# One fused two-layer block on one core: gain rows and x loaded differently at the start, work moved across four chunk boundaries, output stored by chunks

## The chip, the cores and the metric

The kernel runs on one core of one Trainium2 chip. The metric is the device time of one execution in microseconds (us), the median of several runs. One launch computes the whole function.

## What is computed

Two blocks follow each other on a 256 x 2048 float32 activation. The first block has one wide input projection, two attention branches (MLA and differential), a gated merge, an output projection, and a PEER layer with 16384 experts. The second block has an even mixer (retention and a short convolution) and an odd mixer (windowed attention with sinks).

```python
h = rmsnorm(x, g_norm1[l]);  proj = h @ w_in[l]
y_a = mla_branch(proj, ...) @ w_o_mla[l]
y_b = diff_branch(proj, ...) @ w_o_diff[l]
merged = gates[..., :D_MODEL] * y_a + gates[..., D_MODEL:] * y_b
x = x + merged @ w_out[l]
x = x + peer_ffn(rmsnorm(x, g_norm2[l]), w_q_peer[l], sub_keys[l], expert_u[l], expert_v[l])
x = rmsnorm(x, g_final)
# second block
x = x + even_mixer(rms_norm(x, ev_norm_w[0]), ev_w_in[0], ev_conv_w[0], ev_w_out[0], pos)
x = x + odd_mixer(rms_norm(x, od_norm_w[0]), od_w_in[0], ..., od_w_out[0], pos)   # qk-norm, rope, gate = silu
```

## The kernel before

All weights are streamed once, as 1025 blocks of 128 x 1024 float32 (512 KB; the eight blocks of `w_narrow` are 128 x 640), in the order of the table `STREAM`: `w_narrow`, `w_att`, `w_gate`, `w_uq`, `w_ukv`, `w_ob`, `w_oa`, `w_out`, `w_qp`, `w_u`, `w_v`, `w_ein`, `w_eout`, `w_oin`, `w_oout`. SyncE's queue (SP) issues the loads into four `raw` slots. A slot is loaded again once VectorE has read it.

Every block goes through the same chain, which keeps float32 precision. ScalarE writes `hi` (the block rounded to fp32r, L1047), VectorE writes `lo` = raw - hi (L1464), each in two halves, and TensorE multiplies hi*hi, lo*hi and hi*lo (L589, L590, L591): 12 matmuls of 512 columns for a block. There are two `hi`/`lo` slots, so ScalarE can split block b+1 only when TensorE has left block b-1. The activations stand transposed in `xt`, also as hi and lo. They come from TensorE transposes of pairs of tiles (`turn_pair`, L559), and ScalarE and VectorE take them out of the bank (`plain_pair`, or `gain_pair` with the norm's gain, L1082 and L1524).

Each of the engines runs one list that is written out by hand. `gemm` walks over the chunks (512 output columns) and over the blocks of a chunk. VectorE's `take` moves a finished chunk out of its two banks, and adds 1 to `chunk_out`. All other work (norms, rope, softmax, gates) is placed by `beside...(slot)` between two splits; `slot` counts the blocks. `feed(q)` places the takes of transposed pairs, and `LATE` names the pairs that only exist once a chunk has been finished.

The places that the change touches are these. At the start TensorE waits for the identity matrix and all five rows of norm gains, which GpSimd's queue (POOL) loads, and transposes the gains (L703). Then pairs 0 to 2 of x are turned and the eight blocks of `w_narrow` follow; beside them ScalarE squares x for the norm (L1117), one token tile of 128 x 2048 at slot 2 and one at slot 4. In `w_oa`, VectorE's `take_a` runs four operations at each of four chunk ends (L1830, L1831). Between `w_ein` and `w_eout`, and between `w_oin` and `w_oout`, ScalarE applies Silu to the last chunk and VectorE multiplies it in (L1689) ahead of its next split. In `w_oin`, TensorE turns the keys (`turn_qk`, L980) after blocks 14 and 15, into one bank, and VectorE copies them out (`take_qk`, L2233) at its slots 16 and 17. VectorE's slot s stands behind its split of block s+1. At the end, the whole output (2 MB) is stored by one transfer from GpSimd's queue (L467).

```python
if slot in (14, 15):                 # TensorE, beside_oin
    if slot == 14:
        pe.wait_ge(tm_ready, ready.next())
    turn_qk(pairs("swa")[8 + slot - 14])
if slot in (16, 17):                 # VectorE, beside_oin
    take_qk(8 + slot - 16)
```

## Time and profile before

| | |
|---|---|
| median of 3 runs | 3107.28 us (3105.11 to 3108.09) |
| the profiled execution | 3105.93 us |
| its span in the trace | 3103.9 us |
| TensorE matmuls busy | 3052.5 us (98%) |
| VectorE, ScalarE, GpSimd busy | 2024.4 us (65%), 1501.4 us (48%), 567.7 us (18%) |
| mean DMA rate | 189 GB/s |

The profiled execution took 2.0 us more than its span, which the trace does not see. It lies 1.35 us below the median of the runs. Times below are counted from the span's start.

### The profile page before, as it was taken

The page shows a single profiled execution, that of the slowest core. Times are in us where ns is not written, and L with a number is a line of the kernel's source. Part 1 is how long each engine was busy: PE and PEld are TensorE (multiplying, and loading weights), DVE is VectorE, ACT ScalarE, POOL GpSimd, SP SyncE. Part 2 cuts the span into 40 slices and gives each one's busy share as a digit, 9 for nine tenths or more (in the row PEclk, how much of TensorE's full clock was granted, in tenths as well). Part 3 has the DMA queues.
Part 4 walks back from the last instruction along what each step waited for, and adds up shares of the span by engine and source line. Part 5 has one row for each costly group of instructions (what it writes and reads, how often), then busy time and mean ns, then how long its engine had stood idle before and what let it go on. Part 6 is the DMA issues. An engine that isn't in the chain of part 4 may idle for free.

```text
span 3103.9 us, 44769 instructions
## 1 busy us (share of the span) xinstructions
PE 3052.5 (98%) x14773; PEld 2493.2 (80%) x14773; DVE 2024.4 (65%) x3615; ACT 1501.4 (48%) x2443; POOL 567.7 (18%) x341
## 2 busy tenths in 40 slices
PE   7999999999999999999999999999999999999998
PEld 6888787788888888888877777777778888877787
DVE  4567677656877777655555555555576676568864
ACT  4445464455545454544444444444464445556553
POOL 1000000000088878887000000000000000000000
PEclk9999999999999999999999999999999999999999
DMA  6877554466577777776666666676666555653355
GB/s 227 251 258 241 166 163 142 159 187 206 170 183 180 182 183 183 182 185 189 222 224 210 209 206 213 209 231 202 187 191 192 176 170 177 198 167 122 110 157 167
DMA packets 197194, 587.97 MB, mean 189 GB/s; under 512 B 54608, under 2 KB 54736, under 8 KB 195776
## 3 DMA queue, kind: packets, MB, share of 16 engines
q1 hardware_dynamic: 148688, 537.99, 55.7%
q0 software_dynamic: 48368, 48.20, 7.5%
q8 instruction: 80, 1.31, 0.2%
q14 instruction: 58, 0.48, 0.0%
HBM read 565.00 MB, written 21.10 MB: 189 GB/s over the span
## 4 chain that ended last, share of the span: by engine, by line
PE 57%; DVE 1%; issue 0%; ACT 0%; POOL 0%; DVEq 0%; ACTq 0%
PE bank L884 8%; PE bank L589 8%; PE bank L886 8%; PE bank L885 8%; PE bank L591 8%; PE bank L590 8%; PE bank L814 6%; PE bank L815 3%; PE bank L654 1%; PE bank L559 1%; PE bank L666 0%; DVE lo L1464 0%; PE bank L676 0%; PE bank L677 0%; PE bank L675 0%
## 5 line engine op out<-in xcount | busy, mean ns | idle before, releaser
L1464 DVE TENSOR_TENSOR lo<-raw,hi 128x512 fp32r<-128x512 f32 (+2 forms) x1530 | 1313.6, 870 | 930.6 <-ACT hi L1047 920.1
L1047 ACT ACTIVATE hi<-raw 128x512 fp32r<-128x512 f32 (+2 forms) x1530 | 1181.7, 775 | 1482.4 <-PE bank L591 638.4
L814 PE MATMUL bank<-xt,hi 128*128 128x512 f32 x2304 | 818.8, 399 | 5.5 <-DVE lo L1464 4.8
L589 PE MATMUL bank<-hi,xt 128*128 128x512 f32 (+1 forms) x1924 | 768.2, 399 | 13.9 <-DVE lo L1464 13.6
L591 PE MATMUL bank<-hi,xt 128*128 128x512 f32 (+1 forms) x1924 | 751.4, 391 | 0.0
L590 PE MATMUL bank<-lo,xt 128*128 128x512 f32 (+1 forms) x1924 | 749.8, 390 | 0.0
L815 PE MATMUL bank<-xt,lo 128*128 128x256 f32 x2304 | 645.2, 280 | 0.0
L435 POOL DMA_INDIRECT gates_scratch<-picked,place x256 | 507.6, 1983 | 257.2 <-DVE picked L1961 148.9
L814 PEld LDWEIGHTS bank<-xt,hi 128*128 128x128 f32 x2304 | 432.2, 188 | 123.0 <-issue 18.8
L589 PEld LDWEIGHTS bank<-hi,xt 128*128 128x128 f32 x1924 | 363.7, 189 | 96.6 <-issue 21.8
L815 PEld LDWEIGHTS bank<-xt,lo 128*128 128x128 f32 x2304 | 434.9, 189 | 0.0
L591 PEld LDWEIGHTS bank<-hi,xt 128*128 128x128 f32 x1924 | 363.1, 189 | 76.9
L590 PEld LDWEIGHTS bank<-lo,xt 128*128 128x128 f32 x1924 | 364.0, 189 | 69.8
L884 PE MATMUL bank<-hi,w_hi 128*128 128x512 f32 x1024 | 406.7, 397 | 1.9 <-issue 1.8
L886 PE MATMUL bank<-hi,w_lo 128*128 128x512 f32 x1024 | 406.0, 397 | 0.0
L885 PE MATMUL bank<-lo,w_hi 128*128 128x512 f32 x1024 | 405.1, 396 | 0.0
L884 PEld LDWEIGHTS bank<-hi,w_hi 128*128 128x128 f32 x1024 | 192.2, 188 | 81.2 <-DVE lo L1464 42.1
L886 PEld LDWEIGHTS bank<-hi,w_lo 128*128 128x128 f32 x1024 | 192.7, 188 | 46.4
L885 PEld LDWEIGHTS bank<-lo,w_hi 128*128 128x128 f32 x1024 | 193.2, 189 | 35.5
L445 POOL DMA_DIRECT2D xt<-gates_scratch x31 | 23.2, 751 | 569.8 <-DVE hall L1660 506.3
L467 POOL DMA_DIRECT2D out<-hall x1 | 0.7, 717 | 456.4 <-DVEq L2337 456.4
L394 POOL DMA_DIRECT2D hall<-in_q_norm x1 | 0.5, 540 | 377.5 <-DVEq L2213 377.5
(215 smaller groups left out, 1657.8 us busy)
## 6 DMA issues: line engine op xcount, KB each, us to landing
raw<-in_w_u SPq DMA_DIRECT2D x256, 512.0 KB, 3.6
raw<-in_w_v SPq DMA_DIRECT2D x256, 512.0 KB, 3.6
raw<-in_w_ein SPq DMA_DIRECT2D x128, 512.0 KB, 4.0
raw<-in_w_oin SPq DMA_DIRECT2D x72, 512.0 KB, 3.6
raw<-in_w_att SPq DMA_DIRECT2D x64, 512.0 KB, 4.3
raw<-in_w_gate SPq DMA_DIRECT2D x64, 512.0 KB, 3.8
gates_scratch<-u_low POOLq DMA_DIRECT2D x16, 1024.0 KB, 7.6
raw<-in_w_out SPq DMA_DIRECT2D x32, 512.0 KB, 3.9
```

The costliest lines, as they stand in the source:

```text
L435: gp.indirect_dma_start(cells, bass.IndirectOffsetOnAxis(ap=place[:, c:c + 1], axis=0), picked[:, c:c + 1], None, compute_op=ALU.add).then ...
L559: mm = pe.transpose(dst[:, k * T + t * P:k * T + t * P + P], tile[t], ident[:, :])
L589: pe.matmul(acc, xh, h_[:, s], start=first, stop=False)
L590: pe.matmul(acc, xh, l_[:, s], start=False, stop=False)
L591: mm = pe.matmul(acc, xl, h_[:, s], start=False, stop=last)
L814: pe.matmul(acc[:, :], h_[:, s], xt[:, tile].rearrange("p w t -> p (w t)"), start=first, stop=False)
L815: return pe.matmul(acc[:, 0:T], l_[:, s], xt_hi[:, tile], start=False, stop=last)
L884: pe.matmul(acc, wh, h_[:, s], start=first, stop=False)
L885: pe.matmul(acc, wh, l_[:, s], start=False, stop=False)
L886: mm = pe.matmul(acc, wl, h_[:, s], start=False, stop=last)
L1047: act.activation(hi[d][:, c], raw[s][:, c], ACT.Copy).then_inc(hi_ready, 2 // parts)
L1464: dve.tensor_tensor(lo[d][:, c], raw[s][:, c], hi[d][:, c].bitcast(F32), ALU.subtract)\
```

## The change

Seven things are moved or split; no arithmetic is added or left out.

1. Start, loads: the five gain rows go through ScalarE's queue, that of the first norm (`g_norm1`) first and with its own semaphore. The first 512 columns of x are loaded as two halves, before and after the first weight block.
2. Start, gains: TensorE turns only the first norm's 16 columns before the pairs of x, the other 64 after `w_narrow`. ScalarE does a one-element Copy before the first block is there. VectorE copies the first gain before its first split.
3. x is squared at slots 1 and 3 of `w_att`, not at slots 2 and 4 of `w_narrow`; the root moves from slot 6 there to slot 5 of `w_att`.
4. `w_oa`: VectorE takes the second token tile out behind the first split of the next chunk (`spread=True`).
5. `w_eout` and `w_oout`: Silu and product move behind the first and the second split of these products.
6. `w_oin`: the keys are turned after blocks 16 and 17, and copied at VectorE's slots 17 and 18.
7. End: SyncE's queue stores chunks 0 to 2 of the output behind the loads of blocks 14, 22 and 30 of `w_oout`; the last chunk goes as one token tile from SyncE's and one from ScalarE's queue.

```diff
+            def load_x(q, part=0, parts=1):
+                n = W // parts
+                s = slice(q * W + part * n, q * W + part * n + n)
...
+            def store(c):
+                s = slice(c * W, c * W + W)
+                sp.wait_ge(chunk_out, FIRST_CHUNK["w_oout"] + c + 1)
+                sp.dma_start(out.rearrange("(t p) d -> p t d", p=P)[:, :, s], X3[:, :, s]).then_inc(out_saved, 16)
+
+            load_x(0, 0, 2)
             load("w_narrow", 0, None, 0)
+            load_x(0, 1, 2)
...
+                if name == "w_oout":
+                    for b in range(n):
+                        load(name, b, None, 0)
+                        if b in (14, 22, 30):
+                            store(b // 8 - 1)
+                    continue
...
+            sp.wait_ge(last_out, 1)
+            sp.dma_start(out[0:P, 3 * W:4 * W], X3[:, 0, 3 * W:4 * W]).then_inc(out_saved, 16)
+            sp.wait_ge(out_saved, 16 * 5)
...
-            gp.wait_ge(region_free, freed.next())
-            gp.dma_start(out.rearrange("(t p) d -> p t d", p=P), X3).then_inc(out_saved, 16)
-            gp.wait_ge(out_saved, 16)
...
             pe.wait_ge(side[0], SIDE_N[0])
+            pe.wait_ge(gain_in, 16)
+            pe.transpose(bank[6][:, 0:16], gain_rows[64:80, :], ident[64:80, 64:80]).then_inc(gains_turned, 1)
...
             pe.wait_ge(side[10], SIDE_N[10])
-            pe.transpose(bank[6][:, 0:80], gain_rows[0:80, :], ident[0:80, 0:80]).then_inc(gains_turned, 1)
...
+            pe.transpose(bank[7][:, 0:64], gain_rows[0:64, :], ident[0:64, 0:64]).then_inc(gains_turned, 1)
             gemm("w_att", head=2)
...
-                if slot in (14, 15):
-                    if slot == 14:
+                if slot in (16, 17):
+                    if slot == 16:
                         pe.wait_ge(tm_ready, ready.next())
-                    turn_qk(pairs("swa")[8 + slot - 14])
+                    turn_qk(pairs("swa")[8 + slot - 16])
...
+            act.dma_start(gain_rows[64:80, :], a["g_norm1"].rearrange("o (k p) -> (o k) p", p=P)).then_inc(gain_in, 16)
+            for k, g in enumerate(("g_norm2", "g_even", "g_odd", "g_final")):
+                act.dma_start(gain_rows[16 * k:16 * k + 16, :], a[g].rearrange("o (k p) -> (o k) p", p=P))\
+                   .then_inc(side[10], 16)
             act.wait_ge(norm_in, 1)
+            done(act.activation(root[:, 0:1], eps[:, 0:1], ACT.Copy))
...
-            gemm("w_narrow", tail=1, beside=beside_narrow, feed=whole(lambda j: gain_pair("w_narrow", G_H1, j)))
-            gemm("w_att")
+            gemm("w_narrow", feed=whole(lambda j: gain_pair("w_narrow", G_H1, j)))
+            gemm("w_att", head=2, beside_head=head_att)
...
+            def feed_o3(q):
+
+                if q == 0:
+                    silu(P3[:, :, 4096:4608], FIRST_CHUNK["w_oin"] + 8)
+                if q in LATE["o3"]:
+                    plain_pair("w_oout", LATE["o3"][q])
...
+            act.wait_ge(last_out, 2)
+            act.dma_start(out[P:2 * P, 3 * W:4 * W], X3[:, 1, 3 * W:4 * W]).then_inc(out_saved, 16)
...
                         split(b + q, i, 2 * nb, width if q < nb - 1 else BLOCK, 1 if width < BLOCK and q < nb - 1 else 2)
+                        while owed:
+                            owed.pop(0)()
...
-                    for t in range(2):
-                        ins = take(c, i, t, bank[2 * (g % 2) + t])
+                    ins = take(c, i, 0, bank[2 * (g % 2)])
+                    if spread:
+                        owed.append(lambda: take(c, i, 1, bank[2 * (g % 2) + 1]).then_inc(chunk_out, 1))
+                        return
+                    ins = take(c, i, 1, bank[2 * (g % 2) + 1])
...
-            gemm("w_oa", take_a, tail=4, beside=beside_oa)
+            gemm("w_oa", take_a, tail=4, beside=beside_oa, spread=True)
...
+                if q == -1:
+                    plain_pair("w_eout", 5)
+                if q == 1:
+                    dve.wait_ge(act_out, gives.next())
+                    done(mul(O2[:, :, 512:1024], P2[:, :, 3584:4096]))
+                    ready()
...
-                if slot in (16, 17):
-                    take_qk(8 + slot - 16)
+                if slot in (17, 18):
+                    take_qk(8 + slot - 17)
```

ScalarE's queue in `w_narrow`, before, around the two squares (`ACTIVATE hall,ss<-hall`; `xt<-bank` are the takes of turned pairs, `hi<-raw` the splits):

```order
L1082 ACTIVATE xt<-bank4,gain 128x256 [waits turned]
L1082 ACTIVATE xt<-bank4,gain 128x256
L1117 ACTIVATE hall,ss<-hall 128x2048
L1047 ACTIVATE hi0<-raw0 128x640 [waits block_used,raw_loaded0]
L1082 ACTIVATE xt<-bank5,gain 128x256 [waits turned]
```

The same queue now, in `w_att`:

```order
L1064 ACTIVATE hi0<-raw2 128x512 [waits block_used,raw_loaded2]
L1064 ACTIVATE hi0<-raw2 128x512 [waits block_used]
L1134 ACTIVATE hall,ss<-hall 128x2048 [waits x_in3,x_in2,x_in4,x_in1,x_in0]
L1064 ACTIVATE hi1<-raw3 128x512 [waits block_used,raw_loaded3]
L1064 ACTIVATE hi1<-raw3 128x512 [waits block_used]
```

The square has left the stretch with narrow blocks and pairs, and stands between two splits of full blocks.

VectorE's queue in `w_oin` before, from the end of the chunk with the keys and values (`hall<-bank7` is the copy of turned keys):

```order
L2329 TENSOR_SCALAR hall<-bank2,rs 128x512 [waits block_used]
L2329 TENSOR_SCALAR hall<-bank3,rs 128x512
L1464 TENSOR_TENSOR lo0<-raw2,hi0 128x512 [waits hi_ready] x2
L2233 COPY hall<-bank7 128x512 [waits qk_turned]
L2237 TENSOR_TENSOR hall<-hall 128x8x32 [waits chunk_out]
L2239 TENSOR_TENSOR hall<-hall 128x8x32
L1464 TENSOR_TENSOR lo1<-raw3,hi1 128x512 [waits hi_ready,dve_step]
L1464 TENSOR_TENSOR lo1<-raw3,hi1 128x512 [waits hi_ready]
L2233 COPY hall<-bank7 128x512 [waits qk_turned]
```

The same place now:

```order
L2387 TENSOR_SCALAR hall<-bank2,rs 128x512 [waits block_used]
L2387 TENSOR_SCALAR hall<-bank3,rs 128x512
L1503 TENSOR_TENSOR lo0<-raw2,hi0 128x512 [waits hi_ready] x2
L2295 TENSOR_TENSOR hall<-hall 128x8x32 [waits chunk_out]
L2297 TENSOR_TENSOR hall<-hall 128x8x32
L1503 TENSOR_TENSOR lo1<-raw3,hi1 128x512 [waits hi_ready,dve_step]
L1503 TENSOR_TENSOR lo1<-raw3,hi1 128x512 [waits hi_ready]
L2291 COPY hall<-bank7 128x512 [waits qk_turned]
```

Each copy now stands one split later.

VectorE's queue from `w_oin` to `w_oout`, before (`hall<-hall 128x2x512` is the product with the gate):

```order
L2329 TENSOR_SCALAR hall<-bank0,rs 128x512 [waits block_used]
L2329 TENSOR_SCALAR hall<-bank1,rs 128x512
L1689 TENSOR_TENSOR hall<-hall 128x2x512 [waits act_out]
L1464 TENSOR_TENSOR lo0<-raw2,hi0 128x512 [waits dve_step,hi_ready]
L1464 TENSOR_TENSOR lo0<-raw2,hi0 128x512 [waits hi_ready]
```

And now:

```order
L2387 TENSOR_SCALAR hall<-bank0,rs 128x512 [waits block_used]
L2387 TENSOR_SCALAR hall<-bank1,rs 128x512
L1503 TENSOR_TENSOR lo0<-raw2,hi0 128x512 [waits hi_ready] x2
L1503 TENSOR_TENSOR lo1<-raw3,hi1 128x512 [waits hi_ready] x2
L1739 TENSOR_TENSOR hall<-hall 128x2x512 [waits act_out]
```

Two splits now stand ahead of the product; the first pair that needs it is turned by TensorE before block 3.

## Rows read from the trace of the kernel before

**Rows 1.** The page, part 1: busy us (share of the span) by engine
```profile
PE 3052.5 (98%) x14773; PEld 2493.2 (80%) x14773; DVE 2024.4 (65%) x3615; ACT 1501.4 (48%) x2443; POOL 567.7 (18%) x341
```

**Rows 2.** Timeline of the start: start us, duration us, engine, line, tiles, [idle before <-releaser]
```profile
1.27 0.68 POOL L389 DMA_DIRECT2D ident<-in_ident  x1 [0.82 <-POOLq L2412]
...
10.12 0.37 PE L703 MATMUL bank<-ident,u_low 80*128 80x80 f32 x1 [10.12 <-DMA u_low<-in_g_final]
...
14.07 0.61 PE L589 MATMUL bank<-hi,xt 128*128 128x320 f32 x1
...
15.40 0.74 ACT L1047 ACTIVATE hi<-raw 128x640 fp32r<-128x640 f32 x1
...
17.73 0.39 PE L589 MATMUL bank<-hi,xt 128*128 128x320 f32 x1
```

**Rows 3.** Landings: ident (last column, us); the narrow load issued at 3.40
```profile
ident<-in_ident POOLq DMA_DIRECT2D x1, 64.0 KB, 5.4
...
L340 SPq DMA_DIRECT2D raw<-in_w_narrow x1: 772/772/772, 3.4 to 3.4; - x1
...
DMA to landing us min/median/max: 11.9/11.9/11.9
```

**Rows 4.** Timeline, the rest of w_narrow
```profile
23.84 1.91 ACT L1117 ACTIVATE hall<-hall 128x2048 f32<-128x2048 f32 x1
...
27.54 0.60 PE L589 MATMUL bank<-hi,xt 128*128 128x320 f32 x1 [2.26 <-DVE lo L1464]
...
35.98 0.39 PE L589 MATMUL bank<-hi,xt 128*128 128x320 f32 x1 [2.71 <-DVE lo L1464]
```

**Rows 5.** Windows: stretch, us, PE, PEld, DVE, ACT, POOL busy (x), PEclk, DMA, GB/s
```profile
27.54:30.96 3.42, 3.42 (x13) 3.38 (x14) 1.37 (x3) 0.28 (x1) 0.00 (x0) 0.50 0.56 163
35.98:37.79 1.81, 1.81 (x12) 1.81 (x13) 0.58 (x1) 1.14 (x2) 0.00 (x0) 1.00 0.35 81
2771.87:2778.70 6.83, 5.84 (x16) 4.78 (x17) 2.29 (x5) 0.95 (x2) 0.00 (x0) 0.50 0.29 79
3007.39:3010.80 3.41, 3.41 (x9) 2.65 (x9) 1.16 (x2) 0.75 (x2) 0.00 (x0) 0.50 0.80 257
39.57:45.00 5.43, 5.43 (x26) 4.49 (x25) 4.77 (x11) 3.05 (x5) 0.00 (x0) 1.00 0.75 208
...
2779.00:2800.00 21.00, 21.00 (x97) 16.92 (x96) 16.26 (x28) 9.68 (x16) 0.00 (x0) 1.00 0.54 162
```

**Rows 6.** w_oa: TensorE's waits from 565 to 615 (us, times, longest); one taking-out operation
```profile
PE bank L589 <- DVE lo L1464: 3.0, 4, 0.8
...
568.70 0.69 DVE L1830 TENSOR_TENSOR hall<-bank,hall 128x512 f32<-128x512 f32 x1 [1.36 <-PE bank L591]
```

**Rows 7.** Timeline, first wait of TensorE in w_eout
```profile
2636.13 0.47 PE L589 MATMUL bank<-hi,xt 128*128 128x512 f32 x1 [1.68 <-DVE lo L1464]
```

**Rows 8.** Timeline, turning of the keys in w_oin
```profile
2772.12 0.68 DVE L2233 COPY hall<-bank 128x512 f32<-128x512 f32 x1
...
2772.86 1.11 PE L980 MATMUL bank<-ident,hall 128*128 128x128 f32 x4 [3.31 <-DVE hall L2233]
```

**Rows 9.** Timeline, from w_oin to w_oout: Silu, product, TensorE
```profile
3002.90 1.06 ACT L1352 ACTIVATE hall<-hall 128x1024 f32<-128x1024 f32 x1 [3.52 <-DVE hall L2329]
...
3003.99 1.23 DVE L1689 TENSOR_TENSOR hall<-hall 128x1024 f32<-128x1024 f32 x1 [1.12 <-ACT hall L1352]
...
3006.20 0.47 PE L589 MATMUL bank<-hi,xt 128*128 128x512 f32 x1 [2.06 <-DVE lo L1464]
```

**Rows 10.** The end: timeline; landings of the output and of a 320 KB load
```profile
3093.41 1.29 DVE L2211 TENSOR_TENSOR hall<-bank,hall 128x512 f32<-128x512 f32 x2 [4.08 <-PE bank L591]
3095.05 0.72 POOL L467 DMA_DIRECT2D out<-hall  x1 [456.38 <-DVEq L2337]
...
out<-hall POOLq DMA_DIRECT2D x1, 2048.0 KB, 6.8
...
raw<-in_w_narrow SPq DMA_DIRECT2D x1, 320.0 KB, 2.8
```

More of the change, by code:

```diff
@@ L1403, in beside_eout @@
                     gain_pair("w_oin", G_H4, slot - 25)
-            gemm("w_eout", tail=4, beside=beside_eout, feed=late("even", lambda j: plain_pair("w_eout", 4 + j)))
+            gemm("w_eout", tail=4, beside=beside_eout, feed=feed_even)
             exp, take = attention_steps(2)
@@ L1465, in split, with gemm @@
                        .then_inc(lo_ready, 2 // parts)
-            def gemm(name, take, head=0, tail=0, beside=None, beside_head=None, feed=None):
+            owed = []
+            def gemm(name, take, head=0, tail=0, beside=None, beside_head=None, feed=None, spread=False):
                 n, nb = GEMMS[name]
@@ L1673, in head_att @@
             def head_att(slot):
-                if slot == 1:
+                if slot == 2:
+                    dve.wait_ge(gains_turned, 2)
+                    done(dve.tensor_copy(gain[:, 16:80], bank[7][:, 0:64]))
+                    done(dve.tensor_tensor(gain[:, G_E:G_E + 16], gain[:, G_E:G_E + 16], gain[:, G_F:G_F + 16], ALU.mult))
+                    dve.sem_inc(gains_ready, 1)
+                if slot == 6:
                     root_to(rs_h1)
@@ L2222, in _ @@
                 op0=ALU.mult, op1=ALU.add), tail=4, beside=beside_eout,
-                feed=late("even", lambda j: plain_pair("w_eout", 4 + j)))
+                feed=feed_even)
             mask, take = attention_steps(2)
@@ L2331, in _, with feed_o3, add_last @@
             gemm("w_oin", take_oin, tail=9, beside=beside_oin, feed=late("h4", lambda j: gain_pair("w_oin", G_H4, j)))
-            dve.wait_ge(act_out, gives.next())
-            done(mul(O3[:, :, 1536:2048], P3[:, :, 4096:4608]))
-            ready()
-            gemm("w_oout", add_x3, feed=late("o3", lambda j: plain_pair("w_oout", j)))
+            def feed_o3(q):
+                if q == 1:
+                    dve.wait_ge(act_out, gives.next())
+                    done(mul(O3[:, :, 1536:2048], P3[:, :, 4096:4608]))
+                    ready()
+                if q in LATE["o3"]:
+                    plain_pair("w_oout", LATE["o3"][q])
+            def add_last(c, i, t, acc):
+                ins = add_x3(c, i, t, acc)
+                if c == 3 and t == 0:
+                    ins.then_inc(last_out, 1)
+                return ins
+            gemm("w_oout", add_last, feed=feed_o3)
             dve.wait_ge(chunk_out, FIRST_CHUNK["w_oout"] + 4)
-            dve.sem_inc(region_free, 1)
+            dve.sem_inc(last_out, 1)
 def _blocks(w, width=W):
```

65 lines of the change are left out of this document (34 added, 31 removed).

## The prediction, written before the changed kernel ran

> **What bounds the kernel now.** I first read the busy shares. TensorE's matmuls fill 98% of the span and nobody else comes near [rows 1], so the change, which leaves every matmul in place, can only give back the 51 us in which TensorE stands still (3103.9 - 3052.5) and stretches in which it runs at half its clock. I then went through TensorE's timeline for every row with an idle time in front, and the windows around them for the granted clock. Nearly all the stillness that is not spread thinly lies where the change works: 10.1 us before the first instruction [rows 2], waits of 2.26 and 2.71 us in the narrow blocks [rows 4], four waits of together 3.0 us in `w_oa` [rows 6], 1.68 us in `w_eout` [rows 7], 3.31 us at the keys [rows 8], 2.06 us in `w_oout` [rows 9], and the 10.5 us from the last matmul (about 3093.4) to the end [rows 10].
>
> Three of these gaps cost more than they show. The windows behind them stand at PEclk 0.50, that is 1.2 instead of 2.4 GHz: 3.42 us after the wait that ended at 27.54, 6.83 us around the key wait (5.84 of them busy), 3.41 us after the one in `w_oout` [rows 5]. Twelve narrow matmuls took about 3.4 us there against 1.81 us at full clock [rows 5], so half of the busy time in such a window is lost: 1.6, 2.9 and 1.7 us.
>
> **Start.** The transposes need the identity matrix and the first gain row. The identity is issued at 1.27 and lands 5.4 us later, at 6.7 [rows 2, 3]. The gain row's price on ScalarE's queue is not in the trace. Its issue can stand at about 1 us, and the landing is between 2.8 us (320 KB on a hardware queue, [rows 10]) and the 5.4 us of the identity; in either case it is there by 6.7, and I take no cost. TensorE's first instruction so moves from 10.12 to 6.8. The first block's matmuls followed 3.95 us later (14.07, [rows 2]), and so come at about 10.7; at half pace they last 3.3 us, as the next block's 17.73 - 14.07 shows (3.66 with the transposes, [rows 2]), until about 14.4. Then weights are missing: the second narrow block was issued at 3.40 and landed 11.9 us later, at 15.3 [rows 3], and ScalarE split it at 15.40 [rows 2]. The same bytes are ahead of it now, and one issue more, so I put its landing at 15.3 to 15.8. Split (0.74), VectorE's part (about 0.8) and hand-offs put the second block at 17.1 to 17.6, against 17.73. Of 3.3 us gained, **0.4** is left; the rest becomes a gap of some 2 us in front of the second block. What such a gap does to the clock is undecided: after 2.26 us it fell, after 2.71 us it did not [rows 4, 5]. A fall costs 1.6 us on the next block; I charge half, **-0.8**.
>
> **Squares.** A square holds ScalarE for 2.1 us (1.91 and the read of its sum) between a pair and the next split [rows 4]. Without it the split is 2 us earlier. The next thing late is then the chain pair, split, VectorE's split (0.84 + 0.74 + 0.8 and hand-offs, 2.65 us from the end of a transpose), against 2.4 us of TensorE's own work for a narrow block. That leaves 0.3 us of the first wait and 0.7 of the second: **+1.95** and **+2.0**, and **+1.6** for the clock. In `w_att` a block takes TensorE 2.7 us (two in 5.43, [rows 5]) and ScalarE 1.3 us. With a square ScalarE needs 3.4 us once, but it works a block ahead: the split comes up to 2 us later than it could, and is needed 2.7 us later than it could. The cover is 0.7 us, twice; gone, it would cost that much. The late turning of the other gains adds about 0.2 us on TensorE. Start and squares together: 0.4 - 0.8 + 1.95 + 2.0 + 1.6 - 0.2 = **5.0 us** (bounds 2 and 8: the second block's weights 2 us later, or 1.5 earlier with no fall of the clock).
>
> **`w_oa`.** At each chunk end VectorE ran four operations of 0.69 us [rows 6] before a split. With two, the split is 1.4 us earlier, and the wait was 0.7 to 0.8. The other two stand behind the split, with the next needed 2.7 us later. The bank is given back some 4.3 us after the chunk's end; its first reader, a merged pair, is turned 5.4 us after it. **+3.0 us** (bounds 2 and 3).
>
> **`w_eout`, `w_oout`.** Silu (1.06) and product (1.23) stood in a row ahead of the split [rows 9]. Now the chunk is taken out (1.4 us), split 1 follows and its first half is ready about 2.2 us after the chunk's end, needed at 2.7. Split 2 is ready at 4.7, needed at 5.4; the product ends at 7.2, split 3 at 7.9, needed at 8.2, and TensorE asks for the product at the same 8.2. In `w_eout` the taking of pair 5 stands in front, which leaves 0.1 us there. **+1.6** for `w_eout` [rows 7] and 2.06 + 1.7 = **+3.7** for `w_oout` [rows 9, 5] (bounds: half of each, the whole of each).
>
> **Keys.** TensorE wanted to turn the second pair after block 15, into a bank that VectorE copied out only behind two take-outs and a split [rows 8]. Now both turns and copies are one or two blocks later, and the copy ends about 0.6 us before TensorE asks. The second copy joins VectorE's norm work of slot 18. VectorE was busy 16.26 of 21.00 us in this stretch [rows 5], so it has room, but by my count its split of block 21 comes 0.3 us late. 3.31 + 2.9 - 0.3 = **+5.9 us** (bounds 3 and 6.2).
>
> **Stores.** SyncE's queue waits for chunk c behind the load of block 14, 22 or 30. That load itself waits for VectorE's split of block 10, 18 or 26, and VectorE takes the chunk out before block 9, 17 or 25. The wait is therefore over when it is reached, and the weights queued behind it lose one issue (0.45 us), covered by four slots. At the end, before: last addition done at 3094.7, issue at 3095.05, landing 6.8 us later, end of the span 2.0 after [rows 10]. Now: the first token tile goes at 3094.1, the second at about 3094.9. A transfer of 256 KB is not in the trace: it takes no less than 1.6 us and no more than 3.6 (a 512 KB load), and is nearest to the 2.8 us of 320 KB [rows 10]. I take 2.7: landing at 3097.6, end 3099.7. **+4.2 us** (bounds 3.3 and 5.3).
>
> **Sum.** 5.0 + 3.0 + 1.6 + 3.7 + 5.9 + 4.2 = 23.4 us. Against the profiled execution (3105.9) that is 3082.5; the median of the runs lies 1.4 us above it, and I predict for the median: 3107.3 - 23.4 = **3083.9 us**.
>
> **A rule on the clock.** The rows give 6.2 us of the sum to the clock (1.6 + 2.9 + 1.7). The Trainium skill (TensorE: Matmul & The Clock Gate, Part 1: The HAM clock gate) says that the observation behind the clock does not restart with the kernel, so that the moment of a change, and whether a given gap meets it, varies from run to run. The trace agrees in that 2.71 us did not lower the clock where 2.06 did [rows 4, 5, 9]. By the rule alone the clock's part need not return.
>
> **Rivals.**
> - *All gaps close, as summed.* 3079 to 3088. For it: each moved piece has a counted cover. Chance 0.60.
> - *The start gives nothing.* The first weights are bound by transfer: the second block lands 2 us later because x comes in smaller pieces and the queues mix, TensorE idles longer at the front, and the clock falls there. For it: the 11.9 us of [rows 3]; against it: the squares' waits are independent. 3083.9 + 5 = 3089. Chance 0.13.
> - *The clock's part stays.* As under the rule: other gaps (some of 1.5 us remain) meet the low clock instead. 3083.9 + 6.2 = 3090. Chance 0.08.
> - *The waits come back at the next place.* VectorE's covers are 0.1 to 0.7 us. If the product in `w_eout` and `w_oout` and the key work delay a later split, half of 1.6 + 3.7 + 5.9 + 3.0 and a part of the squares return. 3083.9 + 9 = 3093, up to 3099. Chance 0.11.
> - *No net change.* The gaps move and none closes; only the tail is better. 3103. Chance 0.05.
> - *Slower: a store blocks the loads.* If a store stood in SyncE's queue before its chunk is out, the loads behind it would wait up to a chunk's rest. Four slots cover about 10 us; it decides once a store waits over 10 + 23/3, some 18 us, at each of the three places, a chunk's end 22 us ahead. 3107.3 + 3 x (22 - 10) - 23 = 3120. Against it: the order of waits above. Chance 0.03.
>
> **Numbers.** Within 0.2% (6 us), which is about what a measurement of this kernel can tell from none, is 3101 to 3113.5. Faster 0.92, same 0.05, slower 0.03. The range 3079 to 3092 takes in the likeliest case, the two next to it and the beginning of the fourth, 0.8 together; the likeliest one's own is 3079 to 3088.
>
> **What would show it.** In the changed profile: TensorE's first instruction near 6.8; a gap before the second narrow block with ScalarE's split released by a DMA; no wait over 1 us in the rest of `w_narrow`, and the first 512-column matmul near 34.5 instead of 39.57; no waits of `w_oa`; key turns, `w_eout` and `w_oout` without a wait over 0.4 us, and PEclk 1.00 around them; 6.3 us from last matmul to end instead of 10.5. The prediction fails if the first half of `w_att` shows new waits on ScalarE, if VectorE's idle time near the keys is gone and TensorE waits for `lo` there, or if a load lands late behind a store.

## The result, and the profile after

The changed kernel takes **3079.26 us** (median of 4 runs, 3078.20 to 3080.74), the kernel before beside it 3106.76 us (4 runs, 3105.11 to 3108.09). The ratio is 0.9914, with a 95% interval of 0.9901 to 0.9926: 27.5 us less. The prediction was 3083.9 (3079 to 3092), so the time lies 0.3 us above the lower end of the range, and two of the four runs (3078.20 and 3078.42) lie below it. The sum was made against the profiled execution, so it is checked there: 3080.09 us after, with a span of 3078.3, against 3105.93 and 3103.9. The span lost 25.6 us where 23.4 were forecast.

The page, part 1, of the changed kernel, to be held against [rows 1]:

```profile
PE 3047.7 (99%) x14774; PEld 2492.5 (81%) x14774; DVE 2023.4 (66%) x3616; ACT 1501.2 (49%) x2444; POOL 554.1 (18%) x335
```

TensorE now stands still for 30.6 us (3078.3 - 3047.7) instead of 51. Its busy time fell too, by 4.8 us, with one instruction more. Work at half clock is most of that: by my estimate it cost 6.1 us in the kernel before (1.5, 2.9 and 1.7, behind its three long waits) and costs 2.8 here.

The start (timeline, as in [rows 2] and [rows 4]; the last column is the idle time before, and who ended it):

```profile
5.10 0.28 PE L716 MATMUL bank<-ident,u_low 16*128 16x16 f32 x1 [5.10 <-DMA ident<-in_ident]
...
9.01 1.11 PE L572 MATMUL bank<-ident,hall 128*128 128x128 f32 x4 [1.59 <-DMA hall<-in_x]
...
15.75 0.74 ACT L1064 ACTIVATE hi<-raw 128x640 fp32r<-128x640 f32 x1 [4.75 <-DMA raw<-in_w_narrow]
...
17.56 0.60 PE L602 MATMUL bank<-hi,xt 128*128 128x320 f32 x1 [3.70 <-DVE lo L1503]
```

TensorE begins 5 us earlier (at 5.10, where 6.8 was forecast: the identity matrix landed 3.8 us after its issue and not 5.4) and has done the first narrow block by 13.9, but the second block's weights are there only at 15.75, and its matmuls start where they started before (17.56 against 17.73). The five microseconds have become a gap of 3.70.

Windows over the places of [rows 5] to [rows 9], and two wider ones (stretch, us, then busy us and instructions of PE, PEld, DVE, ACT, POOL; PEclk, DMA share, GB/s):

```profile
17.56:21.00 3.44, 3.44 (x13) 3.40 (x14) 1.37 (x3) 0.28 (x1) 0.00 (x0) 0.50 0.58 162
560.00:612.00 52.00, 52.00 (x246) 43.01 (x245) 38.11 (x60) 26.36 (x44) 0.00 (x0) 1.00 0.65 204
2622.00:2634.00 12.00, 12.00 (x58) 9.92 (x57) 9.07 (x14) 6.64 (x11) 3.17 (x6) 1.00 0.58 164
2742.00:2768.00 26.00, 26.00 (x120) 21.50 (x120) 20.93 (x43) 13.24 (x23) 0.00 (x0) 1.00 0.64 199
2975.00:2990.00 15.00, 15.00 (x74) 12.39 (x73) 10.73 (x17) 8.56 (x15) 0.00 (x0) 1.00 0.50 145
...
2600.00:2700.00 100.00, 100.00 (x462) 82.80 (x461) 65.17 (x101) 54.86 (x97) 3.17 (x6) 1.00 0.61 189
...
2737.00:3073.40 336.40, 335.63 (x1643) 268.89 (x1643) 246.94 (x555) 185.51 (x385) 0.00 (x0) 1.00 0.48 149
```

Rows two to five are `w_oa`, `w_eout`, the keys and `w_oout`: TensorE is busy for the whole of each stretch, at full clock. All seven waits there are gone. The last two rows take in what follows, with the blocks in front of which TensorE asks for the two products: it stands still for 0 and for 0.8 us, and the 0.8 are two waits of the softmax that the kernel before has too. The first row is the price of the new gap: 1.2 GHz behind it.

One thing about the clock column must be known for the start. It reads 1.00 until the trace's first record of the clock, also where nothing runs; the pace tells more. In almost all of the first narrow block a matmul of 320 columns starts every 0.27 us in every trace of this case, and at full clock one starts every 0.15 us. The 0.27 is also the pace behind the new gap, where the column says 0.50: TensorE starts at half clock, although the column says 1.00.

The end, against [rows 10] (timeline, and the landings of the last two stores; the last column is us from issue to landing):

```profile
3073.42 0.39 PE L604 MATMUL bank<-hi,xt 128*128 128x512 f32 x1
3073.84 1.29 DVE L2270 TENSOR_TENSOR hall<-bank,hall 128x512 f32<-128x512 f32 x2 [4.08 <-PE bank L604]
3074.56 0.34 SPq L400 DMA_DIRECT2D out<-hall  x1
3075.22 0.37 ACTq L1479 DMA_DIRECT2D out<-hall  x1
```

```profile
out<-hall SPq DMA_DIRECT2D x1, 256.0 KB, 2.5
out<-hall ACTq DMA_DIRECT2D x1, 256.0 KB, 2.7
```

The second store lands at 3075.22 + 2.7 = 3077.9, and the span ends 0.4 us later, at 3078.3.

Since the matmuls keep their pace at full clock, the start times of the same matmuls in the two traces give a balance by stage. Each line is the length of a stretch between two such marks, before less after:

| stretch | measured, us | forecast, us |
|---|---|---|
| start to the first 512-column matmul (39.57, now 36.60) | 3.0 | 5.0 |
| `w_oa`, four chunk ends | 4.1 | 3.0 |
| `w_eout` | 2.0 | 1.6 |
| keys in `w_oin` | 6.2 | 5.9 |
| `w_oout` | 4.0 | 3.7 |
| last matmul to the end (10.9, now 4.9) | 6.0 | 4.2 |
| elsewhere | 0.3 | 0 |
| together | 25.6 | 23.4 |

### The profile page after: what moved, and what is told of

It is laid out like the page before. It is cut to its first block, busy times and chain, and to the rows that moved or that the text cites. A ratio compares the mean times of both kernels' runs of the same rounds, so it can differ in the third digit from the quotient of the medians.

```text
span 3078.3 us, 44643 instructions
## 1 busy us (share of the span) xinstructions
PE 3047.7 (99%) x14774; PEld 2492.5 (81%) x14774; DVE 2023.4 (66%) x3616; ACT 1501.2 (49%) x2444; POOL 554.1 (18%) x335
## 4 chain that ended last, share of the span: by engine, by line
PE 57%; DVE 1%; DMA 0%; ACT 0%; issue 0%; SPq 0%; DVEq 0%; ACTq 0%
PE bank L602 8%; PE bank L604 8%; PE bank L603 8%; PE bank L903 8%; PE bank L902 8%; PE bank L901 8%; PE bank L831 6%; PE bank L832 3%; PE bank L667 1%; PE bank L572 1%; PE bank L679 0%; DMA raw<-in_w_v 0%; DVE lo L1503 0%; PE bank L690 0%; PE bank L689 0%; PE bank L688 0%
## 5 line engine op out<-in xcount | busy, mean ns | idle before, releaser
L452 POOL DMA_INDIRECT gates_scratch<-picked,place x256 | 497.2, 1942 | 259.0 <-DVE picked L2011 154.6
L433 POOL DMA_DIRECT2D gates_scratch<-u_low x16 | 17.8, 1115 | 278.1 <-PE bank L604 278.1
```

The source lines that it names most:

```text
L452: gp.indirect_dma_start(cells, bass.IndirectOffsetOnAxis(ap=place[:, c:c + 1], axis=0), picked[:, c:c + 1], None, compute_op=ALU.add).then ...
```

## The experiments

The theory at this point, A: each part gives what its own stretch shows, and adds up with the others; a wait costs about 0.3 us more than its idle column says; the end gained more than forecast because GpSimd's queue has a cost of its own; the start is bound by the second narrow block's weights. The rival, B, in each expectation, is that the part gives what the idle column says or nothing. The first six kernels are the kernel before with one part alone (e6 with parts 1 and 2), and e7 is the kernel before with its store on another queue; e8, e9 and e11 are the changed kernel with one edit, e10 is e8 with one. The kernel before ran beside them: medians of 3105.92 (30 runs) for the first four, 3105.55 (25 runs) for the next four, and 3106.04 (13 runs) for the last three.

**Part 4 alone, `w_oa` (e1).**

```diff
-                    for t in range(2):
-                        ins = take(c, i, t, bank[2 * (g % 2) + t])
+                    ins = take(c, i, 0, bank[2 * (g % 2)])
+                    if spread:
+                        owed.append(lambda: take(c, i, 1, bank[2 * (g % 2) + 1]).then_inc(chunk_out, 1))
+                        return
+                    ins = take(c, i, 1, bank[2 * (g % 2) + 1])
```

> The kernel before with part 4 alone (VectorE takes the second token tile of a w_oa chunk behind the next split). In the changed kernel the four waits of w_oa are gone, and TensorE stood 4.1 us further ahead after w_oa than before it, while the four waits' idle times add up to 3.0. Theory A: a wait costs TensorE more than the idle time in front of the row, since that counts from the modelled end of the matmul before it and the first matmul after a wait is itself slower; start to start a boundary lost about 1.0 us. Then this kernel alone gives 4.1 us in the trace, all of it between 565 and 615. Theory B: the surplus came from another part of the change (squares, loads). Then it gives 3.0 here.

Measured: 3102.07 us, ratio 0.9989 (0.9979 to 0.9998). The distance between the turnings of one merged pair and the next, a chunk apart, is 11.84 us instead of 12.87, four times: 4.1 us, where the idle column summed to 3.0 [rows 6]. Why the column shows less can be seen at one chunk end of the kernel before (timeline, weight loads left out):

```profile
570.76 0.39 PE L590 MATMUL bank<-lo,xt 128*128 128x512 f32 x1
570.99 0.39 PE L591 MATMUL bank<-hi,xt 128*128 128x512 f32 x1
572.10 0.50 PE L589 MATMUL bank<-hi,xt 128*128 128x512 f32 x1 [0.72 <-DVE lo L1464]
572.43 0.39 PE L590 MATMUL bank<-lo,xt 128*128 128x512 f32 x1
```

In an unbroken row of matmuls one starts every 0.23 us, though each is listed with 0.39: they overlap. Across the gap it is 1.11 us from start to start, then 0.33 to the next. The idle column counts only from the listed end (570.99 + 0.39) to the start, 0.72. What is lost is (1.11 - 0.23) + (0.33 - 0.23) = 0.98. Theory A holds.

**Part 6 alone, the keys (e2).** The diff is the one shown with the change: turns at slots 16 and 17, copies at 17 and 18.

> The kernel before with part 6 alone (keys turned after blocks 16 and 17). Theory A: the wait of 3.31 us and the stretch of 6.8 us at half clock behind it both go, less 0.0 to 0.3 us: 6.0 to 6.4 us in the trace, PEclk 1.00 from 2765 to 2785. Theory B (the clock's part stays): the wait goes, the half-clock stretch shows up near by, and the gain is about 3.3. Theory C (VectorE becomes late in slots 17 to 20): new waits on lo in the 10 us behind, gain under 5.

Measured: 3100.97 us, ratio 0.9986 (0.9976 to 0.9995). The stretch from the last pair turned ahead of the keys to the first one turned behind (2730.35 to 2982.04 before) fell from 251.69 to 245.50 us, by 6.2. All waits of TensorE in it, from 2731 to 2977:

```profile
PE bank L654 <- DVE nmax L1619: 0.8, 2, 0.5
```

Those two belong to the softmax and stand in every kernel here. The 0.3 us that I had charged for a late split of block 21 never appears. Theory A, as measured against this one trace of the kernel before. Seven traces have the wait of 3.31 us, and the clock fell around it in all seven, but not for equally long: for 6.8 us in the kernel before, e3 and e6, for 3.4 us in e1, e4, e5 and e7. One of the latter, e7:

```profile
2774.95:2778.36 3.41, 3.41 (x10) 2.63 (x9) 0.34 (x1) 0.63 (x1) 0.00 (x0) 0.50 0.39 144
2778.36:2781.80 3.44, 3.44 (x17) 2.81 (x16) 2.28 (x5) 1.26 (x2) 0.00 (x0) 1.00 0.04 13
```

In these four the same stretch is 250.5 to 250.6 us long. All of them do the same work at the keys. So the keys' part is worth 6.2 us against the longer fall and 5.1 against the shorter one.

**Part 5 alone, Silu and product (e3).** The diff is shortened to `w_oout`; `w_eout` is edited alike.

```diff
+            def feed_o3(q):
+                if q == 1:
+                    dve.wait_ge(act_out, gives.next())
+                    done(mul(O3[:, :, 1536:2048], P3[:, :, 4096:4608]))
+                    ready()
```

> The kernel before with part 5 alone (Silu and product behind the first and second split of w_eout and w_oout). Theory A: w_eout gives 1.9 to 2.0 (idle 1.68 and the restart), w_oout 3.9 to 4.0 (2.06, restart, 1.7 for the clock), together 5.9 us. Theory B (waits come back at block 3, where the first pair with the product is turned): a wait there in either, together under 4.

Measured: 3101.01 us, ratio 0.9983 (0.9973 to 0.9992). `w_eout` gave 2.0 us and `w_oout` 4.0: the distance between two turned pairs on either side of the boundary fell from 13.81 to 11.85 and from 15.31 to 11.35 us. The window over the place of [rows 9] in this kernel:

```profile
2998.00:3010.00 12.00, 12.00 (x59) 9.93 (x57) 8.81 (x13) 6.58 (x11) 0.00 (x0) 1.00 0.54 173
```

No wait, no half clock, and TensorE has no wait in the 80 us behind it either. Theory A.

**Part 7 alone, the stores (e4).** The diff is the one shown with the change.

> The kernel before with part 7 alone (output by chunks, last two stores from SyncE's and ScalarE's queues). In the changed kernel the time from the start of the last matmul to the end of the span fell from 10.9 to 4.9 us. Theory A: that is this part alone: 6.0 us, of which 4.3 are in issue and landing and 1.7 in the time between the last landing and the span's end (2.05 before, 0.4 after), and the three earlier stores cost nothing. Theory B: the three stores delay loads in w_oout and some of it is lost again: a wait of TensorE there, and less than 5.5 us.

Measured: 3098.26 us, ratio 0.9976 (0.9966 to 0.9986). From the last matmul (3094.02) to the end (3098.9) it is 4.9 us, so 6.0 less. From the first late pair of `w_oout` to the last matmul it is 79.61 us, against 79.62 in the kernel before: three chunk stores between the loads cost TensorE nothing there. Theory A. The median fell by 7.7 us, more than the trace's 6.0; the interval of the ratio reaches from 4.3 to 10.6 us, so the trace decides.

**Part 3 alone, the squares (e5).**

```diff
-                if slot in (2, 4):
-                    t = slot // 2 - 1
-                    if t:
+                if slot in (1, 3):
+                    t = slot // 2
+                    if t == 0:
...
-            gemm("w_narrow", tail=1, beside=beside_narrow, feed=whole(lambda j: gain_pair("w_narrow", G_H1, j)))
-            gemm("w_att")
+            gemm("w_narrow", feed=whole(lambda j: gain_pair("w_narrow", G_H1, j)))
+            gemm("w_att", head=2, beside_head=head_att)
```

> The kernel before with part 3 alone (x squared in w_att), the gains and x loaded as before. In the kernel before the first 512-column matmul starts at 39.57, in the changed one at 36.60. Theory A: the squares alone are worth more than that, 1.95 + 2.0 + 1.6 (two waits less a rest of 0.3 and 0.7, and the half clock behind the first), and the first 512-column matmul starts at 34.0 to 34.6; no new wait in w_att. Theory B: both parts add up, and the squares alone give about 1.5 to 2.5: 37 to 38.

Measured: 3100.43 us, ratio 0.9983 (0.9974 to 0.9993). The first 512-column matmul stands at 34.87, 4.7 us earlier than before and 0.3 later than the end of theory A's range. Theory A. TensorE's waits from 0 to 41:

```profile
PE bank L703 <- DMA u_low<-in_g_final: 10.1, 1, 10.1
PE bank L589 <- DVE lo L1464: 1.7, 3, 0.9
PE bank L559 <- DVE xt L1524: 1.1, 1, 1.1
```

Of the waits in the narrow blocks 1.7 us is left, in three pieces of at most 0.9; the two long ones alone had been 5.0. Once the clock has risen (at 18.4) it stays up. `w_att` takes the squares without loss: from the first 512-column matmul to the one that stands at 565 us in the kernel before it is 525.4 us, there 525.5. The trace shows one thing more, by chance: in `w_oout`, which this kernel leaves as it was, the wait of 2.07 us stands, but the clock did not fall behind it.

```profile
3001.77:3005.17 3.40, 3.40 (x15) 2.85 (x16) 2.35 (x4) 1.03 (x2) 0.00 (x0) 1.00 0.46 140
```

From the start of the matmul behind that wait to the start of the last one it is 3086.91 - 3001.77 = 85.14 us here, and 3092.99 - 3006.20 = 86.79 us in the kernel before, with the same instructions. The difference, 1.65 us, is the price of the low clock alone in this place; I had charged 1.7.

**Parts 1 and 2 alone, the loads (e6).** The diff is the one shown with the change, without its squares and stores.

> The kernel before with parts 1 and 2 alone (gain rows by ScalarE's queue, first gain alone, x in halves), x squared in w_narrow as before. Theory A: the second narrow block's weights land at 15.5 to 15.8 whatever TensorE does; TensorE starts at 5.1, stands still for some 3.7 us in front of that block and runs it at half clock, so this part by itself is worth nothing or costs up to 2.5 us: first 512-column matmul at 39.5 to 42. Theory B: the early start is worth something on its own: 38 or below.

Measured: 3105.44 us, ratio 0.9998 (0.9988 to 1.0007): no change. The timeline of its start:

```profile
5.70 0.28 PE L711 MATMUL bank<-ident,u_low 16*128 16x16 f32 x1 [5.70 <-DMA ident<-in_ident]
...
16.73 0.60 PE L597 MATMUL bank<-hi,xt 128*128 128x320 f32 x1 [2.56 <-DVE lo L1482]
```

TensorE begins 4.4 us earlier than before and has nothing of it: it waits 2.56 us in front of the second block, and the first 512-column matmul is at 40.49, 0.9 us later than before. The block behind the gap ran at the half pace of the first one (a matmul every 0.27 us), though the clock column reads 1.00 there, and the full pace came only at 21.9; in the kernel before it came at 17.3. Theory A. Part 3 carries the whole gain of the start; in the three traces of the changed start parts 1 and 2 take some of it back (36.60, 35.02 and 35.39 against 34.87).

**The 2 MB store by SyncE's queue (e7).** The kernel before, with its one store on another queue.

```diff
+            sp.wait_ge(last_out, 1)
+            sp.dma_start(out.rearrange("(t p) d -> p t d", p=P), X3).then_inc(out_saved, 16)
+            sp.wait_ge(out_saved, 16)
...
-            gp.wait_ge(region_free, freed.next())
-            gp.dma_start(out.rearrange("(t p) d -> p t d", p=P), X3).then_inc(out_saved, 16)
-            gp.wait_ge(out_saved, 16)
```

> The kernel before with its one 2 MB store moved from GpSimd's queue to SyncE's, nothing else. It tells apart what of the 6.0 us of part 7 is the size of the last transfer and what is the queue. Before: issue 0.36 us behind the last addition, landing 6.8 us later, end of the span 2.05 us after the landing. Theory A: the 2.05 us belong to GpSimd's queue; here the span ends about 0.4 us after the landing and the last matmul to end is 8.9 to 9.4 us instead of 10.9. Theory B: the 2.05 us belong to a large store; it stays, and the end comes within 0.5 us of before.

Measured: 3103.61 us, ratio 0.9992 (0.9982 to 1.0001), which the interval can't tell from no change. The trace is sharper: its issue and landing are

```profile
3093.22 0.39 PE L590 MATMUL bank<-hi,xt 128*128 128x512 f32 x1
3093.64 1.29 DVE L2210 TENSOR_TENSOR hall<-bank,hall 128x512 f32<-128x512 f32 x2 [4.08 <-PE bank L590]
3095.02 0.40 SPq L385 DMA_DIRECT2D out<-hall  x1
```

```profile
out<-hall SPq DMA_DIRECT2D x1, 2048.0 KB, 6.4
```

It lands at 3101.4, and the span ends at 3101.8: 8.6 us after the last matmul instead of 10.9, a little better than theory A's 8.9 to 9.4. Leaving GpSimd out of the end is worth 2.3 us of the 6.0, the smaller last transfers the other 3.7.

**Weights between the quarters of x (e8).** The changed kernel, with the loads of narrow blocks 1 to 3 no longer behind all of x.

```diff
             for q in range(1, 4):
                 load_x(q)
+                load("w_narrow", q, None, 0)
...
-                for b in range(1 if name == "w_narrow" else 0, head):
+                for b in range(4 if name == "w_narrow" else 0, head):
```

> The changed kernel with one edit: SyncE issues the second, third and fourth narrow blocks between the quarters of x instead of behind all of x. Theory A (the 3.7 us gap and the half clock behind it come from the order of bytes in SyncE's queue): the second block lands at 10.5 to 12 instead of 15.7, TensorE goes on from the first block without a wait over 0.3 us, the half clock at the second block is gone, and the first 512-column matmul starts at 31 to 33 instead of 36.6; the whole kernel is 3.5 to 5.5 us faster than the changed one. Theory B (the start is bound by all bytes together, and x then lands too late for pairs 4 to 7): waits on x appear in front of blocks 2 or 4, and the gain is under 2 us.

Measured: **3074.50 us** (4 runs, 3073.78 to 3075.27), ratio to before 0.9899 (0.9882 to 0.9915). That is 4.8 us less than the changed kernel's median, which was not taken beside it; but the slowest run here, 3075.27, is 2.9 us under the fastest there, 3078.20. The first 512-column matmul stands 4.4, 4.7 and 5.9 us earlier than in the three traces of the changed start (35.02, 35.39 and 36.60). It beats both kernels. Timeline of its start, TensorE's rows with a wait, and ScalarE's split of the second block:

```profile
5.74 0.28 PE L717 MATMUL bank<-ident,u_low 16*128 16x16 f32 x1 [5.74 <-DMA ident<-in_ident]
...
9.06 1.09 PE L573 MATMUL bank<-ident,hall 128*128 128x128 f32 x4 [1.14 <-DVE xt L1571]
...
11.15 0.74 ACT L1065 ACTIVATE hi<-raw 128x640 fp32r<-128x640 f32 x1
...
16.59 0.38 PE L603 MATMUL bank<-hi,xt 128*128 128x320 f32 x1 [0.65 <-DVE lo L1504]
```

The second block is split at 11.15 instead of 15.75, with no idle time that a DMA ends; the gap is gone, the second block runs at full pace, and the first 512-column matmul is at 30.66 instead of 36.60. Theory A. The same bytes go through the same queue, in another order.

**Stores too early (e9).** The slower rival of the prediction, tried: the changed kernel with `if b in (8, 16, 24)` in place of `(14, 22, 30)`.

> The changed kernel with its three chunk stores standing behind the loads of blocks 8, 16 and 24 instead of 14, 22 and 30. There the store's wait is not over when SyncE's queue reaches it: the load of block 8 is issued when block 4 has been split, the chunk is taken out only behind block 7, so the queue stands for 10 to 12 us and the weights of blocks 9 to 12 behind it. Theory A (a chunk store costs nothing only while its wait is over before the queue reaches it; otherwise the four slots cover about 10 us and the rest is lost, then the load's own 3 to 4 us and two splits must follow): TensorE waits 3 to 6 us at each of three places in w_oout, with the granted clock likely at 0.50 behind at least one, so 9 to 20 us more than the changed kernel, 3088 to 3099. Theory B (slots cover it wherever it stands): no wait of TensorE over 0.4 us in w_oout and the time of the changed kernel, 3079.

Measured: 3102.03 us, ratio to before 0.9987 (0.9978 to 0.9997): 22.8 us more than the changed kernel, nearly its whole gain. SyncE's queue and TensorE in `w_oout` (who, line, releaser: us in total, times, longest):

```profile
SPq L369 <- DVE hall L2270: 40.5, 3, 14.2
```

```profile
PE bank L602 <- DVE lo L1503: 16.8, 3, 5.7
```

Windows behind the first wait:

```profile
3015.19:3018.60 3.41, 3.41 (x8) 2.73 (x9) 1.82 (x3) 1.40 (x3) 0.00 (x0) 0.50 0.86 302
3018.60:3022.00 3.40, 3.40 (x11) 2.66 (x11) 1.31 (x2) 0.88 (x2) 0.00 (x0) 0.67 0.48 164
```

The queue stands 13.5 us at each store, TensorE 5.6, and each time the clock falls. The stretch from the first late pair to the last matmul is 104.1 us long instead of 79.6: 8.2 us lost a place, of which the waits are about 5.9 (5.6 and the 0.3 that the idle column leaves out) and the clock the rest. Theory A in kind, but dearer than its upper end of 20: I had left the clock out at two of the three places.

**GpSimd's small loads later (e10).** The kernel of e8, in which the six small loads (iota to the lambda rows) wait for the first block.

```diff
             load(ident[:, :], a["ident"], 0)
+            gp.wait_ge(block_used, 2)
             load(iota[:, :], a["iota"], 1)
```

> The kernel with the narrow weights between the quarters of x, and in addition GpSimd's six small loads (0.58 MB: iota, cosines, sines, mask, subln and lambda rows) wait until the first narrow block has been used. In the kernel without this, TensorE's first block started at 9.80, after pair 2 had waited for x until 9.06, and the small loads shared the transfer engines from 2 to 9 us. Theory A (the start is bound by the bytes in flight; pair 2 needs 256 KB + 320 KB + 256 KB + 512 KB of SyncE's queue): without the 0.58 MB the second quarter of x lands 1 to 1.5 us earlier and the first 512-column matmul moves from 30.66 to 29.2 to 29.7; about 3073.3. Theory B (the start is bound by the latency of the queue's own transfers and by the chain pair, ScalarE, VectorE): the first block stays within 0.4 us of 9.80 and the time at 3074.5. In either case the waits in the rest of the narrow stage stay at 0.5 to 0.9 us.

Measured: 3073.98 us (4 runs, 3073.56 to 3075.35), ratio 0.9896 (0.9879 to 0.9912), no different from e8. TensorE's waits up to 40 us:

```profile
PE bank L718 <- DMA ident<-in_ident: 5.6, 1, 5.6
PE bank L604 <- DVE lo L1505: 1.8, 3, 0.9
PE bank L574 <- DMA hall<-in_x: 1.6, 2, 0.9
```

The first block starts at 10.38 and the first 512-column matmul at 30.91, not at 29.5. Theory A is out: without the bytes of GpSimd's queue x came no earlier. Theory B is nearer, but its bound of 0.4 us around 9.80 was missed too (0.58 later), and these runs don't show what does set that time.

**The last 256 KB by GpSimd's queue (e11).**

```diff
-            act.wait_ge(last_out, 2)
-            act.dma_start(out[P:2 * P, 3 * W:4 * W], X3[:, 1, 3 * W:4 * W]).then_inc(out_saved, 16)
...
+            gp.wait_ge(last_out, 2)
+            gp.dma_start(out[P:2 * P, 3 * W:4 * W], X3[:, 1, 3 * W:4 * W]).then_inc(pool_saved, 16)
+            gp.wait_ge(pool_saved, 16)
```

> The changed kernel with the last 256 KB of the output (second token tile of the last chunk) stored by GpSimd's queue instead of ScalarE's; the first tile stays on SyncE's. Read from the last matmul to the end of the span, 4.88 us in the changed kernel. Theory A (GpSimd's queue itself costs some 2 us at the end: 2.05 us from landing to the end of the span in the kernel before, 0.4 with the hardware queues): 6.5 to 7.3 us, most of it between the landing and the end. Theory B (the 2 us belonged to the size of the 2 MB transfer, and a small one has none): 4.9 to 5.3 us.

Measured: 3080.39 us (2 runs), ratio 0.9917 (0.9897 to 0.9937). The last matmul starts at 3072.23 and the span ends at 3079.1, 6.9 us later instead of 4.9. The issue and the landing:

```profile
3074.29 0.55 POOL L485 DMA_DIRECT2D out<-hall  x1 [442.02 <-DVEq L2411]
```

```profile
out<-hall POOLq DMA_DIRECT2D x1, 256.0 KB, 2.7
```

Landing at 3077.0, end 2.1 us behind it. The transfer takes the same 2.7 us as by ScalarE's queue; the 2 us come after it, whatever the size. Theory A, as far as the number goes.

GpSimd's takes 1.70 us and starts 0.2 us after the landing in e11 (3077.19) and in the kernel before (3102.01); it takes 1.70 us at the end of all seven traces in which GpSimd stores last. Where GpSimd has no store at the end (the changed kernel, e4, e7 to e10) the same DRAIN stands at 2626 to 2640 us, and takes 7 to 9 us beside other work; SyncE's, which then closes the kernel, takes 0.01. So 1.7 of the 2.1 us are GpSimd's own closing behind its last wait, and nothing shows that its queue is slow. Whether a store issued by GpSimd and waited for by SyncE would avoid them was not run.

## Why the prediction was right, and where its sizes were off

The likeliest case came true: every gap that the change aims at in the four products closed, none came back at a later place, and the parts add up. Run alone, the seven parts gave 3.9, 5.0, 4.9, 7.7, 5.1 and 0.1 us in medians (parts 4, 6, 5, 7, 3, and 1 with 2), together 26.6 of the 27.5. Each of these medians is uncertain by some 3 us, so that they meet so closely is in part luck; the traces, in the same order, are the better sum: 4.1, 6.2, 6.0, 6.0, 4.7 and -0.9, together 26.1, where the span lost 25.6. That the total came within 2.2 us of its forecast is in part luck too: one term was 2.0 too high, and the others together 4.2 too low. In the terms of the sum:

**Start and squares, 5.0 forecast, 3.0 measured: the term that came out too high.** Its pieces were right but for the clock. They can be read without the idle column, by the distances between the first matmuls of the narrow blocks:

| from | before, us | now, us | gain |
|---|---|---|---|
| span's start to second block | 17.73 | 17.56 | 0.2 |
| second to third | 2.91 | 4.04 | -1.1 |
| third to fourth | 2.19 | 3.12 | -0.9 |
| fourth to fifth (wait 2.26, now 0.47) | 4.71 | 2.91 | 1.8 |
| fifth to sixth (half clock before) | 3.73 | 2.20 | 1.5 |
| sixth to seventh (wait 2.71, now 0.89) | 4.71 | 2.89 | 1.8 |
| seventh to the first 512-column matmul | 3.59 | 3.88 | -0.3 |

The second block was put at 17.1 to 17.6 and came at 17.56, held by the weights as said. The two waits gave 3.6 us for the 3.95 forecast, the clock behind the first 1.5 for 1.6, and the late turning of the gains cost 0.3 for 0.2. But the gap in front of the second block was 3.70 us, not "some 2", since the first block ran 0.9 us earlier than I had put it, and I had charged a fall of the clock on one block at half its chance. It fell, and for two blocks: PEclk 0.50 from 16.8 to 23.6. The two blocks took 7.16 us where two blocks at full pace take 4.4; 0.7 of these 2.8 us had been a wait in front of the third block before, so 2.1 were lost (the 1.1 and 0.9 of the table) for the 0.8 charged. The changed kernel's start was traced twice more, in e9 and e11: there the gap was 2.97 and 2.85 us, the low clock lasted for about one block (3.67 and 3.75 us from the second to the third), and the first 512-column matmul came at 35.02 and 35.39. The term is then 4.6 and 4.2, and 5.0 was closer than the first trace makes it look. e6 and e8 show the mechanism from both sides: without the squares' move the earlier start is worth nothing, and with the weights in time 4.2 of its 4.3 us are kept (30.66 against the 34.87 of e5).

**`w_oa` 3.0, `w_eout` 1.6, `w_oout` 3.7: each too low by what the idle column leaves out.** Six waits, some 0.3 us each: measured 4.1, 2.0 and 4.0. The bounds of `w_oa`, 2 and 3, were wrong for this reason: its upper end was the sum of that column, and the column is not an upper end.

**Keys, 5.9 forecast, 6.2 measured.** The price of the gap and the clock was right for the trace that it was read from; the subtracted 0.3 for a late split was not needed. That the term hit is in part luck: in four of the seven traces with this wait the low clock lasted half as long, and against those the part is worth 5.1.

**Stores, 4.2 forecast, 6.0 measured: the term with the largest miss upward.** The landing of 256 KB was put at 2.7 and measured 2.5 and 2.7. The step that failed is "landing at 3097.6, end 3099.7": I carried the 2.0 us from landing to end over to the other queues. e7 and e11 show that it comes with GpSimd: 0.4 us where SyncE's and ScalarE's queues store last, for 2 MB and for 256 KB; 2.1 with GpSimd's, for 256 KB, of which its closing DRAIN is 1.70. (The lower bound that I gave for the transfer, 1.6 us, rests on no row.) The chunk stores themselves were rightly costed at nothing: in the changed kernel SyncE's queue has no wait at all at its three chunk stores, where it has three of together 40.5 us in e9.

**The rivals.** *The start gives nothing* described what parts 1 and 2 do by themselves (e6), but not the term, which the squares carry. *The clock's part stays* fell: in the changed kernel's trace the clock is full from 23.6 us to the last matmul. What the traces bear out of the rule that I had weighed there (the Trainium skill, TensorE: Matmul & The Clock Gate, Part 1: The HAM clock gate), that the moment of a change varies from run to run, is the wait of 2.07 us in e5, behind which the clock stayed, where the same wait lowered it in the kernel before and in e1, e2, e4, e6 and e7, and the two lengths of the fall at the keys. *Waits come back at the next place* fell: no new wait stands in `w_oout` or at the keys. *Slower: a store blocks the loads* had its mechanism right and its price wrong. I let four slots cover 10 us and put the deciding point at 18 us of standing. In e9 the queue stood 13.5 us and that already cost 8.2 a place, since the cover is 13.5 - 5.6, about 8 us (an estimate from e9 alone), and each gap brought the low clock with it. Three such places are enough to undo the whole change; the choice of block 14 over block 8 is worth nearly as much as the whole change.

## What to carry to other kernels

Price a wait of a pipelined engine by the distance between the starts of the instructions around it, less the usual distance, and add the stretch at half clock behind it; the idle column alone is a lower end (0.72 against 0.98 us in `w_oa`). Where a shorter wait stays in the same place, the restart stays too, and the idle column's difference is right (1.79 and 1.82 us against 1.80 and 1.82 at the start). Starting the bound engine earlier gives nothing until the next thing that it needs is earlier too (e6 gave 0.1 us): follow the loads in the order in which they are consumed, and queue the next blocks' weights between the pieces of x, not behind them (e8 gave 4.8). A store in the queue that feeds the weights was free where its wait was over when it was reached, and cost 8.2 us where the queue stood 13.5 us at it. Keep GpSimd out of the last store: with it the end came 2.0 us later (e11).

## What the runs showed of the hardware that was not expected

The end of a kernel depends on the engine that stores last and waits for it: from landing to the end of the span 2.05 and 2.1 us with GpSimd, whose closing DRAIN takes 1.70 us there, 0.4 with SyncE's or ScalarE's queue and SyncE waiting.

Over ten traces (the kernel before, e1 to e7, e9, e11), TensorE's waits and the clock right behind them: waits of 1.0 to 1.7 us after the first 25 us never lowered it; the one of 2.06 in `w_oout` did in six of seven traces; the one of 3.31 at the keys in all seven that have it, for 3.4 or 6.8 us; those of 5.4 to 5.7 in e9 three times of three. Length alone doesn't decide: the wait of 2.71 us at 35.98 left the clock up in the kernel before, e2, e3, e4 and e7, where the wait of 2.27 some 8 us ahead of it had lowered it for a time, as did one of 2.65 in e6 behind one of 1.98 that had lowered it, and it lowered the clock in e1, where the wait ahead was 1.56 and had not. What the rule behind this is stays open; these runs don't settle it.

Also open is what still holds the first block at 9.8 to 10.4 us in e8 and e10. Traces with the same order of loads differ there too: in the changed start the first block came at 9.78, 10.33 and 10.34 us.
